# Stick-breaking attention: triangular matmuls against a backward VectorE scan

## The chip, the core and the metric

The kernel runs on one core of one Trainium2 chip. Five engines work from queues of their own and meet only through semaphores: TensorE (PE, with its weight loads shown as PEld), VectorE (DVE), ScalarE (ACT), GpSimd (POOL), and SyncE (SP), which here only starts transfers. The metric is the time of one execution on the device, in microseconds (us). Each engine runs its own instructions strictly in order, so an instruction that waits also holds back everything written behind it.

## What is computed

One transformer layer for 512 tokens of width 1024: RMSNorm, one projection, two kinds of attention (8 heads each, width 64), an output projection, a mixture of 32 experts with 4 chosen per token, and a last RMSNorm. The change touches only the stick-breaking heads:

```python
z = einsum('bhqd,bhkd->bhqk', q, k) * scale
strict = q_index > k_index
log_1mb = where(strict, log_sigmoid(-z), 0.0)
suffix = cumsum(log_1mb, axis=keys, reverse=True) - log_1mb
log_a = where(strict, log_sigmoid(z) + suffix, -inf)
out = einsum('bhqk,bhkd->bhqd', exp(log_a), v)
```

With sp = softplus(z) = -log_sigmoid(-z), log_a is z minus the sum of sp over this key and all later keys of the same query. A query tile of 128 sees only the keys up to its own end, so the four tiles of a head hold 128, 256, 384 and 512 keys.

## The kernel before, in words

Every fp32 operand of a matmul is split in two fp32r parts, high and low, and each product is three matmuls (high by high, high by low, low by high). ACT writes the high part, DVE subtracts it to get the low part.

The attention stage is one loop over steps `s` on every engine, 32 steps for 8 pairs of heads: steps 0 to 15 are stick-breaking (`STICK` is 16, four steps a pair), 16 to 31 are forgetting attention. I write i for `s % 4`. Between the attention instructions of a step stand the projection matmuls of later heads, cut in three parts of two or three units (a unit is three 512-column matmuls, L1618 to L1620); this is the fill. Functions `filled`, `finish`, `place` and `turn_part` fix before the run in which part each projection tile is worked on and where ACT and DVE empty it.

Before the change a stick-breaking step works with keys on the partitions:

- PE `z_scores(s)`: the mask matmul and three products a head (L1686, L1690) for two heads, into the PSUM pair `zpair[s % 2]`.
- ACT `softplus_tail(s)`: absolute value, exp, log (L832, L834, L836) of both heads at once into `lbuf`.
- DVE `softplus(s)`: adds max(z, 0) (L1205), copies to the fp32r `sp_hi` (L1210) and subtracts to `sp_lo` (L1211).
- PE `log_a(s-1)`: multiplies `sp_hi` and `sp_lo` of this and all later key tiles by a matrix of -1 (`neg_one`, or triangular `neg_tri`) and adds onto the scores (L1702).
- ACT `stick_exp(s-1)`: exp into `pbuf` (L844). DVE `stick_split(s-1)`: `av_hi`, `av_lo` (L1220, L1222).
- PE `pv_stick(s-2)`: six matmuls with v (L1717) into the PSUM pair `obank`.

After the fourth step of a pair ACT's `mix_evac(1, c)` (L878, L887) and DVE's `mix_lo_part(1, c)` (L1259, L1265) empty `obank`. The queues also hold, in every step but i=3, the split of a weight piece (L757 on ACT, L1127 on DVE) and the emptying of a projection tile (L804, L808, L817 on ACT; L1168, L1174 on DVE). The order on each engine is the order of the code.

Of the kernel before, what the change touches and what calls it, by code (L numbers as in the profile page):

```python
# [129 lines left out]
def build(nc, x, norm1_g, w_in, b_f, g_fox, g_sb, w_out, norm2_g, w_router, b_router, w1, b1, w2, b2,  # L130
# [6 lines left out]
    with ExitStack() as ctx:  # L137
# [27 lines left out]
        neg_tri = sb("neg_tri", [P, P], F32R)  # L165
        neg_one = sb("neg_one", [P, P], F32R)
# [43 lines left out]
        av_hi = in_slot("av_hi", [P, 2, 2, BANK], F32R, 4)  # L210
        av_lo = in_slot("av_lo", [P, 2, 2, BANK], F32R, 5)
# [20 lines left out]
        tri_raw = over("tri_raw", [P, P], F32, room_at)  # L232
        one_raw = over("one_raw", [P, P], F32, room_at + 512)
# [103 lines left out]
        absz, e_ready, ln_ready, sp_raw, sp_ready = (sem(n) for n in ("absz", "e_ready", "ln_ready", "sp_raw", "sp_ready"))  # L337
        loga_ready, a_ready, av_hi_r, av_lo_r, pvs_done = (sem(n) for n in ("loga_ready", "a_ready", "av_hi_ready", "av_lo_ready", "pvs_done"))
        mix_hi, mix_sq, mix_lo, sq_added = sem("mix_hi"), sem("mix_sq"), sem("mix_lo"), sem("sq_added")
        tri_ready = sem("tri_ready")  # L340
# [233 lines left out]
        def _(pool):  # L574
# [34 lines left out]
            constant(choose(maskS, [[1, P]], ALU.is_gt, MASKED, 0, -1))  # L609
# [140 lines left out]
        def _(act):  # L750
# [75 lines left out]
            def softplus_tail(s):  # L826

                n, l = (s % TT + 1) * P, lbuf[:, s % 2]
                act.wait_ge(scored, s + 1)
                if s >= 2:  # L830
                    act.wait_ge(sp_ready, s - 1)
                nc.scalar.activation(l[:, :, 0:n], zpair[s % 2][:, :, 0:n], ACT.Abs).then_inc(absz, 1)  # L832
                act.wait_ge(absz, s + 1)
                nc.scalar.activation(l[:, :, 0:n], l[:, :, 0:n], ACT.Exp, scale=-1.0).then_inc(e_ready, 1)  # L834
                act.wait_ge(e_ready, s + 1)
                nc.scalar.activation(l[:, :, 0:n], l[:, :, 0:n], ACT.Ln, bias=1.0).then_inc(ln_ready, 1)  # L836

            def stick_exp(s):
# [3 lines left out]
                if s >= 2:  # L842
                    act.wait_ge(av_lo_r, s - 1)
                nc.scalar.activation(pbuf[:, s % 2, :, 0:n], zpair[s % 2][:, :, 0:n], ACT.Exp).then_inc(a_ready, 1)  # L844

            def fox_exp(s):
# [4 lines left out]
                if u < 2:  # L851
                    act.wait_ge(av_lo_r, s - 1)
# [8 lines left out]
            def pt_evac(s):  # L861
# [3 lines left out]
                if u < TT:  # L865
                    act.wait_ge(loga_ready, STICK)
# [35 lines left out]
            act.wait_ge(consts, 22)  # L902
# [17 lines left out]
            for s in range(STEPS + 1):  # L920
                evacuate((s, True))
                if s > STICK and s % TT == 1 and s > STICK + TT:
                    mix_evac(0, (s - STICK - TT) // TT)
                if s < STICK:
# [10 lines left out]
                evacuate((s, False))  # L935
                if s == F_STEP + 1:
# [3 lines left out]
                if TT < s < STICK + TT and s % TT == 1:  # L940
                    mix_evac(1, s // TT - 1)
# [173 lines left out]
        def _(dve):  # L1115
# [80 lines left out]
            def sp_cols(i):  # L1196

                return slice(P * i * (i + 1) // 2, P * (i + 1) * (i + 2) // 2)

            def softplus(s):  # L1200

                i = s % TT
                n, l = (i + 1) * P, lbuf[:, s % 2]
                dve.wait_ge(ln_ready, s + 1)
                nc.vector.scalar_tensor_tensor(out=l[:, :, 0:n], in0=zpair[s % 2][:, :, 0:n], scalar=0.0,  # L1205
                                               in1=l[:, :, 0:n], op0=ALU.max, op1=ALU.add).then_inc(sp_raw, 1)
                dve.wait_ge(sp_raw, s + 1)
                if s >= TT:
                    dve.wait_ge(loga_ready, TT * (s // TT))
                chained(nc.vector.tensor_copy(sp_hi[:, :, sp_cols(i)], l[:, :, 0:n]))  # L1210
                nc.vector.tensor_tensor(sp_lo[:, :, sp_cols(i)], l[:, :, 0:n], sp_hi[:, :, sp_cols(i)].bitcast(F32),  # L1211
                                        ALU.subtract).then_inc(sp_ready, 1)

            def stick_split(s):

                n, b = (s % TT + 1) * P, s % 2
                dve.wait_ge(a_ready, s + 1)
                if s >= 2:
                    dve.wait_ge(pvs_done, s - 1)
                nc.vector.tensor_copy(av_hi[:, b, :, 0:n], pbuf[:, b, :, 0:n]).then_inc(av_hi_r, 1)  # L1220
                dve.wait_ge(av_hi_r, s + 1)
                nc.vector.tensor_tensor(av_lo[:, b, :, 0:n], pbuf[:, b, :, 0:n], av_hi[:, b, :, 0:n].bitcast(F32),  # L1222
                                        ALU.subtract).then_inc(av_lo_r, 1)
# [58 lines left out]
            for g in range(1, STAGES):  # L1282
                lo_early(g)
                if g == STAGES - 1:
                    dve.wait_ge(consts, 22)
                    chained(nc.vector.tensor_scalar(seltab[:, 0:E], iotas[:, 0:E], pmod, None, ALU.is_equal))
                    nc.vector.tensor_copy(neg_tri[:], tri_raw[:]).then_inc(tri_ready, 1)
                    nc.vector.tensor_copy(neg_one[:], one_raw[:]).then_inc(tri_ready, 1)
                    nc.vector.tensor_copy(sel8[:], sel_raw[:]).then_inc(tri_ready, 1)
# [27 lines left out]
            for s in range(STEPS + 1):  # L1317
                if s < STICK:
                    lower((s, True))
                    softplus(s)  # L1320
                elif s < STEPS:
                    fox_max(s)
                    lower((s, True))
                    fox_scale(s)
                else:
                    lower((s, True))
                if 1 <= s <= STICK:
                    stick_split(s - 1)
                elif s > STICK:
# [10 lines left out]
                if TT < s < STICK + TT and s % TT == 1:  # L1340
                    mix_lo_part(1, s // TT - 1)
# [273 lines left out]
        def _(pe):  # L1615
# [61 lines left out]
            def z_scores(s):  # L1677

                p, i = divmod(s, TT)
                j, n, zb, b = TT - 1 - i, (i + 1) * P, bank[2 * (s % 2):2 * (s % 2) + 2], p % 2  # L1680
                if s >= 2:
                    pe.wait_ge(a_ready, s - 1)
                if i == 0:
                    pe.wait_ge(proj_lo, 3 * p + 2)
                for m in range(2):
                    pe.matmul(zb[m][:, 0:P], identB[:], maskS, start=True, stop=False, skip_group_check=True)  # L1686
                for w, x in ((k_hi, q_hi), (k_hi, q_lo), (k_lo, q_hi)):
                    for m in range(2):
                        half = slice(64 * m, 64 * m + 64)
                        mm = pe.matmul(zb[m][:, 0:n], w[half, b, j * P:(j + 1) * P], x[half, b, j * P:S],  # L1690
                                       start=False, stop=w is k_lo, skip_group_check=True)
                mm.then_inc(scored, 1)

            def log_a(s):

                i, zb = s % TT, bank[2 * (s % 2):2 * (s % 2) + 2]
                pe.wait_ge(sp_ready, s + 1)
                for v in range(i + 1):
                    o, w = P * v * (v + 1) // 2, P * (v + 1)
                    for m in range(2):  # L1700
                        for part in (sp_hi, sp_lo):
                            mm = pe.matmul(zb[m][:, (i + 1) * P - w:(i + 1) * P], (neg_tri if v == i else neg_one)[:], part[:, m, o:o + w],  # L1702
                                           start=False, stop=v == i and part is sp_lo, skip_group_check=True)
                mm.then_inc(loga_ready, 1)

            def pv_stick(s):

                p, i = divmod(s, TT)
# [367 lines left out]
```

## Time and profile before

| quantity | value |
|---|---|
| median of 3 runs | 1536.88 us (1536.72 to 1537.83) |
| the profiled execution's own time | 1539.24 us |
| its span, first to last instruction | 1537.5 us |
| PE busy | 1482.2 us, 96% |
| DVE busy | 1335.3 us, 87% |
| ACT busy | 1108.4 us, 72% |
| stick-breaking scores begin / forgetting scores begin | 37.51 us / 166.34 us |

Busy shares are means over stages that differ. The attention stage lies between about 37 and 312 us, and from about 359 us on the expert weights stream through. A matmul in the timeline is shown with its whole pipeline (0.39 us for 512 columns), while the next one starts 0.23 us after it; what PE's queue pays for a matmul is the distance of starts, not its duration.

### The profile page before, as it was taken

To read this page: it belongs to the slowest core of one execution; us is meant where nothing else is said; L and a number is where in the kernel's file an instruction comes from. 1 tells how busy PE (TensorE), PEld (TensorE's weight loads), DVE (VectorE), ACT (ScalarE), POOL (GpSimd) and SP (SyncE) were. 2 spreads that over 40 slices of the span, in tenths; PEclk is the share of its full clock that TensorE was granted. 3 is DMA by queue.
4 is the path that set the end of the run, shared out by engine and by line. 5 is a ranking of instruction groups with operands and counts; after the bars stand their busy time and mean duration, and the time that the engine had idled before them with its cause. 6 is when DMAs were issued, how large, how long until landed. Compare 5 with 4: busy or idle time off the path is not lost.

```text
span 1537.5 us, 22435 instructions
## 1 busy us (share of the span) xinstructions
PE 1482.2 (96%) x7120; PEld 1196.7 (78%) x7120; DVE 1335.3 (87%) x1515; ACT 1108.4 (72%) x1314; POOL 257.0 (17%) x203
## 2 busy tenths in 40 slices
PE   6999998889899999999999999999999999999995
PEld 5788786777778788888888888778888888888874
DVE  5477655567999999999999999999999999999996
ACT  5466554254788888888888788888888888878875
POOL 5000000036011121111111211112221111111110
PEclk9999999999999999999999999999999999999998
DMA  8021121169999999999999999999999999999953
GB/s 249 13 82 44 40 82 56 32 231 368 344 368 372 361 363 373 378 351 368 366 377 366 366 366 367 366 359 376 357 376 358 364 374 363 370 372 360 358 200 120
DMA packets 100023, 451.82 MB, mean 294 GB/s; under 512 B 13394, under 2 KB 25682, under 8 KB 67216
## 3 DMA queue, kind: packets, MB, share of 16 engines
q1 hardware_dynamic: 90656, 434.68, 74.8%
q0 software_dynamic: 9328, 16.64, 4.5%
q8 instruction: 22, 0.36, 0.1%
q14 instruction: 17, 0.14, 0.0%
HBM read 445.18 MB, written 22.54 MB: 304 GB/s over the span
## 4 chain that ended last, share of the span: by engine, by line
PE 71%; DVE 17%; issue 7%; ACT 4%; POOL 1%; DVEq 0%; ACTq 0%; POOLq 0%
PE zpair L1979 43%; PE bank L1979 7%; DVE stage_lo L1127 7%; PE bank L1618 4%; PE bank L1619 3%; PE bank L1620 3%; ACT stage_hi L757 3%; DVE qk L1501 2%; DVE act_lo L1475 2%; DVE qk L1497 2%; PE bank L1949 2%; PE zpair L1702 1%; PE zpair L1958 1%; PE bank L1766 1%; PE bank L1717 1%
## 5 line engine op out<-in xcount | busy, mean ns | idle before, releaser
L1127 DVE TENSOR_TENSOR stage_lo<-ring,stage_hi 128x1024 fp32r<-128x1024 f32 x796 | 953.2, 1223 | 51.4 <-ACT stage_hi L757 12.2
L757 ACT CAST stage_hi<-ring 128x1024 fp32r<-128x1024 f32 x796 | 828.9, 1054 | 195.5 <-PE zpair L1979 149.4
L1979 PE MATMUL zpair<-stage_hi,act_hi 128*128 128x512 f32 x1024 | 323.5, 397 | 5.4 <-DVE stage_lo L1127 5.3
L1979 PE MATMUL zpair<-stage_lo,act_hi 128*128 128x512 f32 x1024 | 316.6, 390 | 0.0
L1979 PE MATMUL zpair<-stage_hi,act_lo 128*128 128x512 f32 x1024 | 316.4, 390 | 0.0
L1979 PEld LDWEIGHTS zpair<-stage_hi,act_hi 128*128 128x128 f32 x1024 | 187.4, 188 | 53.8 <-DVE stage_lo L1127 13.8
L1979 PEld LDWEIGHTS zpair<-stage_lo,act_hi 128*128 128x128 f32 x1024 | 192.8, 188 | 40.9
L1979 PEld LDWEIGHTS zpair<-stage_hi,act_lo 128*128 128x128 f32 x1024 | 192.7, 188 | 40.7
L1979 PE MATMUL bank<-stage_hi,act_hi 128*128 128x512 f32 x512 | 164.9, 403 | 7.0 <-DVE stage_lo L1127 4.5
L650 POOL COPY sidx<-gtab 128x1 int32 (+1 forms) x31 | 101.2, 3265 | 392.4 <-ACT qk L1030 392.4
L1979 PE MATMUL bank<-stage_lo,act_hi 128*128 128x512 f32 x512 | 159.2, 392 | 0.0
L1979 PE MATMUL bank<-stage_hi,act_lo 128*128 128x512 f32 x512 | 158.4, 391 | 0.0
L1979 PEld LDWEIGHTS bank<-stage_hi,act_hi 128*128 128x128 f32 x512 | 91.8, 189 | 36.0 <-DVE stage_lo L1127 16.5
L1979 PEld LDWEIGHTS bank<-stage_hi,act_lo 128*128 128x128 f32 x512 | 96.4, 188 | 21.3
L1979 PEld LDWEIGHTS bank<-stage_lo,act_hi 128*128 128x128 f32 x512 | 96.4, 188 | 20.9
L639 POOL COPY gidx<-gtab 128x1 int32 (+1 forms) x31 | 5.7, 185 | 487.4 <-PE bank L1943 487.4
L1475 DVE TENSOR_TENSOR act_lo<-bank,act_hi 128x512 fp32r<-128x512 f32 x128 | 81.9, 681 | 4.9 <-ACT act_hi L1016 3.3
L1618 PE MATMUL bank<-act_hi,stage_hi 128*128 128x512 f32 x192 | 80.2, 418 | 2.9 <-DVE v_lo L1168 2.7
L1619 PE MATMUL bank<-act_lo,stage_hi 128*128 128x512 f32 x192 | 75.8, 395 | 0.0
L1620 PE MATMUL bank<-act_hi,stage_lo 128*128 128x512 f32 x192 | 75.8, 395 | 0.0
L1022 ACT ACTIVATE qk<-qk 128x1024 f32<-128x1024 f32 x32 | 34.0, 1061 | 41.3 <-DVE qk L1497 41.3
L654 POOL DMA_INDIRECT x_scratch<-qk,sidx x31 | 58.3, 1880 | 25.0 <-POOL sidx L650 25.0
(310 smaller groups left out, 1483.7 us busy)
## 6 DMA issues: line engine op xcount, KB each, us to landing
ring<-in_w SPq DMA_DIRECT2D x384, 1024.0 KB, 7.5
ring<-in_w_in SPq DMA_DIRECT2D x12, 1024.0 KB, 5.4
ring<-in_w_out SPq DMA_DIRECT2D x4, 1024.0 KB, 4.8
xs_all<-in_x SPq DMA_DIRECT2D x4, 512.0 KB, 7.7
ring<-in_x SPq DMA_DIRECT2D x4, 512.0 KB, 3.8
tn_scratch<-qk SPq DMA_DIRECT2D x4, 512.0 KB, 2.9
x_scratch<-ring SPq DMA_DIRECT2D x4, 512.0 KB, 4.1
ring<-x_scratch SPq DMA_DIRECT2D x4, 512.0 KB, 5.6
```

Of the source, the lines that this page charges most:

```text
L650: nc.gpsimd.tensor_copy(sidx[:], gtab[:, i:i + 1] if isinstance(i, int) else gtab[:, bass.ds(i, 1)]).then_inc(sidx_copied, 1)
L654: nc.gpsimd.indirect_dma_start(out=x2_d[:, :], out_offset=bass.IndirectOffsetOnAxis(ap=sidx[:, 0:1], axis=0), in_=yout, in_offset=None, bo ...
L757: nc.scalar.copy(dst, src).then_inc(split_hi, 1)
L1022: nc.scalar.activation(sig, glu, ACT.Gelu_apprx_sigmoid).then_inc(sig_done, 1)
L1127: nc.vector.tensor_tensor(dst, src, hi_ap.bitcast(F32), ALU.subtract).then_inc(split_lo, 1)
L1475: nc.vector.tensor_tensor(dst_lo[:, 4 * h:4 * h + n, :], bank[6 + h][:, 0:n * P].rearrange("p (k t) -> p k t", k=n), dst_hi[:, 4 * h:4 * h ...
L1497: ins = nc.vector.tensor_scalar(glu[:, h * BANK:(h + 1) * BANK], bank[h][:], LIMIT, None, ALU.min)
L1501: ins = nc.vector.tensor_scalar(lin[:, h * BANK:(h + 1) * BANK], bank[2 + h][:], LIMIT, -LIMIT, ALU.min, ALU.max)
L1618: pe.matmul(dst, w_hi, m_hi, start=start, stop=False)
L1619: pe.matmul(dst, w_hi, m_lo, start=False, stop=False)
L1620: return pe.matmul(dst, w_lo, m_hi, start=False, stop=stop)
L1979: mm = pe.matmul(bank[b0 + h][:], w[:, k, :], m[:, j % STAGES, h * BANK:(h + 1) * BANK], start=start and w is T_hi and m is stage_hi, stop ...
```

## The change

Queries are put on the partitions and keys along the free dimension, as in the forgetting heads. `log_a` and its 160 matmuls go, with `sp_hi`, `sp_lo`, `av_hi`, `av_lo` and the two constant matrices. In their place:

- DVE `log_weights(s)`: adds max(z, 0) as before, then one `tensor_tensor_scan` a head that runs through the keys backward (step -1) and adds them up, then z minus the sum. It keeps fp32; no split.
- ACT `stick_exp(s)` now reads `lbuf` in SBUF.
- PE `turn_stick(s)`: two times i+1 transposes of `pbuf` into `obank`. It waits until DVE has emptied `obank` of the turned tile before (`st_lo_ready`), and for i=0 until the pair before has left it (`mix_lo`).
- ACT `stick_turned(s)` copies the turned tile to `pt_hi`, one instruction a head; DVE `stick_rest(s)` subtracts to `pt_lo`.
- PE `pv_stick(c)`: once a pair, 24 matmuls with v, with the same columns in all as the four calls before.
- `mix_evac` and `mix_lo_part` of a pair move from the end of the step with i=1 to the front of the step with i=2.

```diff
-            def log_a(s):
-                i, zb = s % TT, bank[2 * (s % 2):2 * (s % 2) + 2]
-                pe.wait_ge(sp_ready, s + 1)
-                for v in range(i + 1):
...
+            def turn_stick(s):
+                c, i = divmod(s, TT)
+                pe.wait_ge(a_ready, s + 1)
+                if i == 0:
+                    wait(pe, mix_lo, 2 * c)
+                else:
+                    pe.wait_ge(st_lo_r, s)
+                for m in range(2):
+                    for kb in range(i + 1):
+                        mm = pe.transpose(obank[m][:, kb * P:(kb + 1) * P], pbuf[:, s % 2, m, kb * P:(kb + 1) * P], identF[:])
+                mm.then_inc(st_turned, 1)
...
+            def pv_stick(c):
+                pe.wait_ge(st_lo_r, TT * (c + 1))
+                pe.wait_ge(proj_lo, 3 * c + 3)
+                weigh(c).then_inc(pvs_done, TT)
...
+            def log_weights(s):
+                n, l = (s % TT + 1) * P, lbuf[:, s % 2]
+                dve.wait_ge(ln_ready, s + 1)
+                chained(nc.vector.scalar_tensor_tensor(out=l[:, :, 0:n], in0=zpair[s % 2][:, :, 0:n], scalar=0.0,
+                                                       in1=l[:, :, 0:n], op0=ALU.max, op1=ALU.add))
+                for m in range(2):
+                    back = l[:, m, 0:n][:, ::-1]
+                    loose(nc.vector.tensor_tensor_scan(back, back, ones[:, 0:1].to_broadcast([P, n]), 0.0, ALU.add, ALU.mult))
+                dve.wait_ge(steps["dve"], count["dve"])
+                nc.vector.tensor_tensor(l[:, :, 0:n], zpair[s % 2][:, :, 0:n], l[:, :, 0:n], ALU.subtract).then_inc(loga_ready, 1)
...
+            def stick_rest(s):
                 i = s % TT
+                dve.wait_ge(st_hi_r, s + 1)
+                for m in range(2):
+                    ins = nc.vector.tensor_tensor(pt_lo[:, m, i:4 * i + 1:3, :], obank[m][:, 0:(i + 1) * P].rearrange("p (k q) -> p k q", q=P),
+                                                  pt_hi[:, m, i:4 * i + 1:3, :].bitcast(F32), ALU.subtract)
+                ins.then_inc(st_lo_r, 1)
...
             for s in range(STEPS + 1):
                 if s < STICK:
                     lower((s, True))
-                    softplus(s)
+                    if s % TT == 2 and s > TT:
+                        mix_lo_part(1, s // TT - 1)
+                    if s >= 2 and s % TT != 2:
+                        stick_rest(s - 2)
+                    log_weights(s)
...
                 if F_STEP <= s < F_STEP + 4 and s != F_STEP + 1:
                     forget_gate((0, None, 1, 2)[s - F_STEP])
-                if TT < s < STICK + TT and s % TT == 1:
-                    mix_lo_part(1, s // TT - 1)
+                if s % TT == 2 and s < STICK:
+                    stick_rest(s - 2)
...
                 for part in range(PARTS):
                     q = PARTS * s + part
-                    if part == 1 and 1 <= s <= STICK:
-                        log_a(s - 1)
+                    if s % TT == 1 and TT < s < STICK + TT and part == (1 if s > STICK else 2):
+                        pv_stick(s // TT - 1)
+                    if part == 2 and s % TT == 2 and s < STICK:
+                        turn_stick(s - 2)
...
+                if 1 <= s <= STICK and s % TT != 1:
+                    turn_stick(s - 1)
```

How the rows move is seen best in step 14, the third one with i=2 after a finished pair. On PE before, from the second part of the step on: the sums of `sp`, then fill, then the products with v of step 12 (after whose six rows come two units of fill and the scores of step 15).

```order
L1702 MATMUL zpair<-sp_hi,neg_one 128x128 [waits sp_ready]
L1702 MATMUL zpair<-sp_lo,neg_one 128x128
L1702 MATMUL zpair<-sp_hi,neg_one 128x128
L1702 MATMUL zpair<-sp_lo,neg_one 128x128
L1702 MATMUL zpair<-sp_hi,neg_tri 128x256
L1702 MATMUL zpair<-sp_lo,neg_tri 128x256
L1702 MATMUL zpair<-sp_hi,neg_tri 128x256
L1702 MATMUL zpair<-sp_lo,neg_tri 128x256
L1618 MATMUL bank<-act_hi,stage_hi 128x512 [waits proj_lo,split_lo]
```

On PE now, the last part of the same step and the start of step 15 (L1705 is `turn_stick`, L1687 the mask matmul of the next scores).

```order
L1705 MATMUL bank<-identF,pbuf 128x128 [waits mix_lo,a_ready]
L1705 MATMUL bank<-identF,pbuf 128x128
L1619 MATMUL bank<-act_hi,stage_hi 128x512
L1620 MATMUL bank<-act_lo,stage_hi 128x512
L1621 MATMUL bank<-act_hi,stage_lo 128x512
L1619 MATMUL bank<-act_hi,stage_hi 128x512
L1620 MATMUL bank<-act_lo,stage_hi 128x512
L1621 MATMUL bank<-act_hi,stage_lo 128x512
L1705 MATMUL bank<-identF,pbuf 128x128 [waits st_lo_ready,a_ready]
L1705 MATMUL bank<-identF,pbuf 128x128 x3
L1687 MATMUL zpair<-masks,identB 128x128 [waits loga_ready]
```

Two turned tiles stand in this one step with a single part of fill between them, and the second waits for DVE.

On DVE before, step 14 from the emptying of the pair (written at the end of step 13) on.

```order
L1259 SCALAR_TENSOR_TENSOR stick_lo<-bank,cols,stick_hi 64x512 [waits mix_sq] x2
L1265 TENSOR_TENSOR f_neg<-f_neg,f_max 128x512 [waits sq_added]
L1205 SCALAR_TENSOR_TENSOR lbuf<-zpair,lbuf 128x2x384 [waits ln_ready]
L1210 CAST sp_hi<-lbuf 128x2x384 [waits loga_ready,sp_raw]
L1211 TENSOR_TENSOR sp_lo<-lbuf,sp_hi 128x2x384 [waits dve_steps]
L1220 CAST av_hi<-pbuf 128x2x256 [waits pvs_done,a_ready]
L1222 TENSOR_TENSOR av_lo<-pbuf,av_hi 128x2x256 [waits av_hi_ready]
L1127 TENSOR_TENSOR stage_lo<-ring,stage_hi 128x1024 [waits split_hi]
L1174 SCALAR_TENSOR_TENSOR k_lo<-bank,k_hi 128x512 [waits scored,proj_hi]
```

On DVE now, the same stretch (L1209 is the scan, L1218 `stick_rest`).

```order
L1256 SCALAR_TENSOR_TENSOR stick_lo<-bank,cols,stick_hi 64x512 [waits mix_sq] x2
L1262 TENSOR_TENSOR f_neg<-f_neg,f_max 128x512 [waits sq_added]
L1205 SCALAR_TENSOR_TENSOR lbuf<-zpair,lbuf 128x2x384 [waits ln_ready]
L1209 SCALAR_TENSOR_TENSOR lbuf<-lbuf,ones 128x384 [waits dve_steps]
L1209 SCALAR_TENSOR_TENSOR lbuf<-lbuf,ones 128x384
L1211 TENSOR_TENSOR lbuf<-zpair,lbuf 128x2x384 [waits dve_steps]
L1132 TENSOR_TENSOR stage_lo<-ring,stage_hi 128x1024 [waits split_hi]
L1179 SCALAR_TENSOR_TENSOR k_lo<-bank,k_hi 128x512 [waits scored,proj_hi]
L1218 TENSOR_TENSOR pt_lo<-bank,pt_hi 128x128 [waits st_hi_ready]
L1218 TENSOR_TENSOR pt_lo<-bank,pt_hi 128x128
```

`stick_rest` of the tile with i=0, for which PE's second turn waits, stands last in DVE's step, behind `log_weights`, the weight piece and the projection tile. ACT's copy of that tile likewise stands last in ACT's step.

## Rows read from the trace of the kernel before

**Rows 1.** The page: span, busy time of each engine, the chain by engine.

```profile
span 1537.5 us, 22435 instructions
PE 1482.2 (96%) x7120; PEld 1196.7 (78%) x7120; DVE 1335.3 (87%) x1515; ACT 1108.4 (72%) x1314; POOL 257.0 (17%) x203
...
PE 71%; DVE 17%; issue 7%; ACT 4%; POOL 1%; DVEq 0%; ACTq 0%; POOLq 0%
```

**Rows 2.** Busy time by stretch: length, PE, PEld, DVE, ACT, POOL, clock, DMA share, GB/s.

```profile
119.65:150.69 31.04, 31.04 (x177) 25.33 (x176) 21.07 (x29) 18.99 (x28) 0.00 (x0) 1.00 0.12 35
37.51:63.75 26.24, 23.54 (x119) 18.60 (x119) 12.02 (x19) 11.62 (x18) 0.00 (x0) 0.93 0.09 32
63.75:95.45 31.70, 31.70 (x179) 26.05 (x179) 21.64 (x31) 19.80 (x29) 0.00 (x0) 1.00 0.22 67
...
157.50:181.73 24.23, 24.23 (x138) 19.97 (x137) 15.78 (x26) 11.89 (x21) 0.00 (x0) 1.00 0.13 44
```

**Rows 3.** The stretch of one pair, line L1702 (`log_a`) alone: length, PE, PEld.

```profile
119.65:150.69 31.04, 6.21 (x40) 5.60 (x40) 1.00 0.12 35
```

**Rows 4.** Timeline of PE, eight transposes of `turn_p` and the fill behind: start, us, what.

```profile
199.56 1.04 PE L1752 MATMUL zpair<-identF,pbuf 128*128 128x128 f32 x8
200.35 0.48 PE L1618 MATMUL bank<-act_hi,stage_hi 128*128 128x512 f32 x1
```

**Rows 5.** Timeline of PE, step 10: fill after `pv_stick`, scores, `log_a`; scores of step 11.

```profile
118.28 0.39 PE L1618 MATMUL bank<-act_hi,stage_hi 128*128 128x512 f32 x1
...
119.65 0.28 PE L1686 MATMUL zpair<-masks,identB 128*128 128x128 bf16 x2
...
122.09 0.22 PE L1702 MATMUL zpair<-sp_hi,neg_one 128*128 128x128 f32 x1
...
126.46 0.29 PE L1686 MATMUL zpair<-masks,identB 128*128 128x128 bf16 x2
```

**Rows 6.** Timeline of ACT, steps 10 and 11.

```profile
122.86 0.85 ACT L836 ACTIVATE lbuf<-lbuf 128x768 f32<-128x768 f32 x1
...
125.03 0.60 ACT L808 ACTIVATE k_hi<-bank 128x512 fp32r<-128x512 f32 x1
...
129.84 1.06 ACT L836 ACTIVATE lbuf<-lbuf 128x1024 f32<-128x1024 f32 x1
```

**Rows 7.** Timeline of DVE, step 10.

```profile
123.74 0.96 DVE L1205 SCALAR_TENSOR_TENSOR lbuf<-zpair,lbuf 128x768 f32<-128x768 f32 x1 [0.96 <-ACT lbuf L836]
...
127.27 1.22 DVE L1127 TENSOR_TENSOR stage_lo<-ring,stage_hi 128x1024 fp32r<-128x1024 f32 x1
128.40 0.68 DVE L1174 SCALAR_TENSOR_TENSOR k_lo<-bank,k_hi 128x512 fp32r<-128x512 f32 x1
```

**Rows 8.** Groups of DVE instructions by shape, 40 to 200 us: busy, mean ns.

```profile
L1211 DVE TENSOR_TENSOR sp_lo<-lbuf,sp_hi 128x768 fp32r<-128x768 f32 x4 | 3.8, 958 | 0.1
...
L1210 DVE CAST sp_hi<-lbuf 128x768 fp32r<-128x768 f32 x4 | 2.2, 560 | 0.1
...
L1187 DVE TENSOR_TENSOR_SCAN f_sum<-f_max,f_neg 128x512 f32<-128x512 f32 x1 | 1.2, 1217 | 0.0
...
L1248 DVE TENSOR_TENSOR pt_lo<-zpair,pt_hi 128x256 fp32r<-128x256 f32 x1 | 0.4, 415 | 0.0
```

**Rows 9.** Timeline of DVE, step 2: the first part of the forget gate.

```profile
64.12 0.75 DVE L1181 TENSOR_SCALAR f_sum<-bank,cols 128x512 f32<-128x512 f32 x1
...
65.51 0.42 DVE L1184 TENSOR_SCALAR f_max<-f_sum 128x512 f32<-128x512 f32 x1
```

**Rows 10.** Timeline of PE around its wait in step 0.

```profile
43.77 0.60 PE L1674 MATMUL bank<-identF,vT 128*128 128x128 f32 x4
47.07 0.76 PE L1618 MATMUL bank<-act_hi,stage_hi 128*128 128x512 f32 x1 [2.70 <-DVE v_lo L1168]
...
50.56 0.40 PE L1620 MATMUL bank<-act_hi,stage_lo 128*128 128x512 f32 x1
```

**Rows 11.** Busy time by stretch, as rows 2, behind that wait.

```profile
47.00:50.00 3.00, 2.93 (x7) 2.38 (x8) 0.52 (x1) 0.00 (x0) 0.00 (x0) 0.51 0.00 0
```

More of the change, by code:

```diff
@@ L842, in stick_exp, with stick_turned @@
                 if s >= 2:
-                    act.wait_ge(av_lo_r, s - 1)
-                nc.scalar.activation(pbuf[:, s % 2, :, 0:n], zpair[s % 2][:, :, 0:n], ACT.Exp).then_inc(a_ready, 1)
+                    act.wait_ge(st_turned, s - 1)
+                nc.scalar.activation(pbuf[:, s % 2, :, 0:n], lbuf[:, s % 2, :, 0:n], ACT.Exp).then_inc(a_ready, 1)
+            def stick_turned(s):
+                i = s % TT
+                act.wait_ge(st_turned, s + 1)
+                if s == 0:
+                    act.wait_ge(sel8_ready, 1)
+                if i == 0:
+                    wait(act, pvs_done, s)
+                for m in range(2):
+                    ins = nc.scalar.copy(pt_hi[:, m, i:4 * i + 1:3, :], obank[m][:, 0:(i + 1) * P].rearrange("p (k q) -> p k q", q=P))
+                ins.then_inc(st_hi_r, 1)
             def fox_exp(s):
@@ L923, in _ @@
                     mix_evac(0, (s - STICK - TT) // TT)
+                if s % TT == 2 and TT < s < STICK + TT:
+                    mix_evac(1, s // TT - 1)
+                if 2 <= s < STICK + 2 and (s - 2) % TT:
+                    stick_turned(s - 2)
                 if s < STICK:
@@ L1339, in _ @@
                     forget_gate((0, None, 1, 2)[s - F_STEP])
-                if TT < s < STICK + TT and s % TT == 1:
-                    mix_lo_part(1, s // TT - 1)
+                if s % TT == 2 and s < STICK:
+                    stick_rest(s - 2)
                 if s > STICK + TT and s % TT == 1:
@@ L1685, in z_scores @@
                 for m in range(2):
-                    pe.matmul(zb[m][:, 0:P], identB[:], maskS, start=True, stop=False, skip_group_check=True)
-                for w, x in ((k_hi, q_hi), (k_hi, q_lo), (k_lo, q_hi)):
+                    pe.matmul(zb[m][:, i * P:(i + 1) * P], identB[:], maskS, start=True, stop=False, skip_group_check=True)
+                for w, x in ((q_hi, k_hi), (q_hi, k_lo), (q_lo, k_hi)):
                     for m in range(2):
                         half = slice(64 * m, 64 * m + 64)
-                        mm = pe.matmul(zb[m][:, 0:n], w[half, b, j * P:(j + 1) * P], x[half, b, j * P:S],
-                                       start=False, stop=w is k_lo, skip_group_check=True)
+                        mm = pe.matmul(zb[m][:, 0:n], w[half, b, i * P:(i + 1) * P], x[half, b, 0:n],
+                                       start=False, stop=w is q_lo, skip_group_check=True)
@@ new lines, in weigh @@
+            def weigh(ph):
+                for kb in range(TT):
+                    for m in range(2):
+                        for w, x in ((v_hi, pt_hi), (v_hi, pt_lo), (v_lo, pt_hi)):
+                            mm = pe.matmul(obank[m][:, kb * P:S], w[:, ph % 2, kb, :],
+                                           x[:, m, 4 * kb:3 * kb + TT, :].rearrange("p i q -> p (i q)"),
+                                           start=kb == 0 and w is v_hi and x is pt_hi, stop=kb == TT - 1 and w is v_lo, skip_group_check=True)
+                return mm
@@ L1762, in pv_fox @@
                     pe.wait_ge(ms_read, 1)
-                for kb in range(TT):
-                    for m in range(2):
-                        for w, x in ((v_hi, pt_hi), (v_hi, pt_lo), (v_lo, pt_hi)):
-                            mm = pe.matmul(obank[m][:, kb * P:S], w[:, ph % 2, kb, :],
-                                           x[:, m, 4 * kb:3 * kb + TT, :].rearrange("p i q -> p (i q)"),
-                                           start=kb == 0 and w is v_hi and x is pt_hi, stop=kb == TT - 1 and w is v_lo, skip_group_check=True)
-                mm.then_inc(pvf_done, 1)
+                weigh(ph).then_inc(pvf_done, 1)
             def sums(kind):
```

98 lines of the change are left out of this document (23 added, 75 removed).

## The prediction, made before the changed kernel ran

> **What bounds the kernel now.** I read the page first: PE is busy 96% of the span and carries 71% of the chain that ended last [rows 1]. A mean over stages says little about one stage, so next came the busy time by stretch. One pair of stick-breaking heads takes 31.04 us, from the scores of step 10 to those of step 14; PE is busy all of it, DVE 21.07 and ACT 18.99 [rows 2]. So each microsecond of PE's queue counts there, and DVE and ACT have 10 and 12 us to spare, as long as PE never waits for them. Then I read the three queues side by side over one step, since the change trades PE work for a longer way through ACT and DVE. A late attention stage is not caught up later: nearly everything behind it hangs on PE too, so I pass the difference on in full.
>
> **What PE gains.** `log_a` goes. Its 40 matmuls a pair are 6.21 us of busy time [rows 3]. They stand in four runs, and each run's last matmul shows 0.39 us where the next starts 0.23 us later (six starts in 1.37 us [rows 5]), so the queue pays 6.21 - 4 x 0.17 = 5.5 us. Twenty transposes a pair come: eight take 0.79 us of the queue [rows 4], so twenty take 2.0. `pv_stick` keeps 24 matmuls a pair and their columns, the scores theirs; I cost both at nothing, being moved on the same engine. If PE never waited, a pair would take 31.04 - 5.5 + 2.0 = 27.5 us, 3.5 less.
>
> **What DVE and ACT get.** Eight subtractions (958 ns at 768 columns [rows 8], 0.83 at the mean width of 640) and eight casts (560 ns at 768, about 0.49) go: 10.5 us a pair. Eight scans come. One forward scan of 512 columns took 1217 ns [rows 8]; at the mean of 320 columns that is 0.82, so 6.5 us. Four subtractions come, 3.3, and eight from PSUM for `pt_lo` (415 ns at 256 columns [rows 8], so about 0.48), 3.9. DVE goes from 21.1 to 24.3 us a pair; ACT gets eight copies, about 3.4 us, and goes to 22.4. Both still fit under 27.5: it is not their work but its place that matters.
>
> No row shows a backward scan or one with a broadcast second operand. Below I bound it by the subtraction of as many columns, 0.69 us at 512; above by twice the forward scan, 2.43. I take the forward scan's 1.22, the nearest row, the same instruction on fp32 in SBUF.
>
> **The wait that comes.** In a step with i=2, PE turns the tile i=0 ahead of its last part of fill, and the tile i=1 right behind that part. `turn_stick` for i=1 waits until DVE has emptied `obank` of the first tile. I follow both sides from the end of `pv_stick`, at 118.28 in step 10 [rows 5].
>
> - ACT empties the pair and then makes abs, exp and log of the new scores: the log ends at 122.86 + 0.85 = 123.71, 5.4 us after the start [rows 6]. DVE now works through max 0.96, two scans of 384 columns 0.95 each, subtraction 0.96 and two handovers 0.1: 3.9. Behind it stand the weight piece (128.40 - 127.27 = 1.1) and the projection tile, 0.65 [rows 7], then the two `pt_lo` subtractions of 128 columns, about 0.28 each. Together 5.4 + 3.9 + 1.1 + 0.7 + 0.6 = 11.7 us. ACT's copy of that tile is ready before this: `k_hi` ends at 125.63 [rows 6], 7.4, and half a microsecond more.
> - PE has fill, scores and a part of fill, 122.09 - 118.28 = 3.8 [rows 5], a second part 1.4, the first turn 0.2, the third part 1.4: 6.8 us.
>
> PE waits 11.7 - 6.8 = 4.9 us. Behind the waiting transpose are queued the scores of the next step, hence ACT's whole next step, so nothing overtakes. The pair takes 27.5 + 4.9 = 32.4 us, 1.4 more than now. The other new waits fall short: from the scores of i=3 the log is done after 129.84 + 1.06 - 126.46 = 4.4 us [rows 5, 6], the log weights after 9.5, the exp after 10.6, and PE comes to that turn after 11.3; the pair's last `pt_lo` is done after 15.3, and PE comes to `pv_stick` after 16.4. This bites three times, in steps 6, 10 and 14: 4.2 us.
>
> **The two ends.** In step 2 no pair has to be emptied, but the first part of the forget gate stands between `log_weights` and `stick_rest`. It begins at 64.12 before [rows 9]; PE's queue loses 0.4 us of `log_a` ahead, and DVE's 3.6 us of softplus and split become 3.9, so it begins at about 64.0, lasts 65.51 + 0.42 - 64.12 = 1.8 us [rows 9], then 0.6 for `pt_lo`, 0.4 for the turn. Step 3 starts at 66.8 instead of 63.75 [rows 2]: 3.1 us later. In step 5 the forget gate's last part delays the squares of the first pair, 0.5 more. From step 15 to 18, PE loses two `log_a` runs (4.2 us) and three `pv_stick` calls (3.1), gains one of 3.75 and 14 transposes, 1.5, and meets waits of 0.9 for the copy of v and 1.7, since the last stick-breaking exp now stands behind the first forgetting exp and DVE's longer log weights: -4.2 - 3.1 + 3.75 + 1.5 + 2.6 is 0.6 on the 24.23 [rows 2]. I give 0.5 of this back in the first forgetting steps, where other waits stand: 0.1.
>
> **The clock.** After a wait of 2.70 us in step 0 the granted clock was 0.51 for 3 us, the 1.2 GHz level [rows 10, 11]. Eight starts took 50.56 - 47.07 = 3.5 us where eight take 1.8 at full clock: 1.6 lost. The new waits are longer, so I add 1.6 four times, 6.4 us; PE stands on the way to every next wait, so the loss isn't hidden.
>
> The Trainium skill (TensorE: Matmul & The Clock Gate, "What's actually happening") advises against such a term: "For modeling, the ramp penalty is <1% of a typical kernel span". By it the sum below would be 7.9 and the time 1544.8. The trace agrees on the size, for 6.4 of 1537.5 us is 0.4%, but against a change of 8 us that is no small term, and I keep it.
>
> **Sum.** 3.1 + 4.2 + 0.5 + 0.1 + 6.4 = 14.3 us. The profiled execution took 1539.24 us, 2.4 more than the median of the runs, so it becomes 1553.5; for the median, 1536.88 + 14.3 = 1551.2. I predict 1551.
>
> **Rivals.**
>
> - PE stays full (the side of faster). Mechanism: `stick_rest` of i=0 is done before PE has finished the third part of fill. It decides at 6.8 us after `pv_stick`, where I find 11.7. Then PE's gain stands: four pairs at 3.5, 14 us, 1523. For it speaks that DVE and ACT have room in every pair; against it that the log alone ends after 5.4 us and DVE's four instructions after another 3.9, both in front of it. Even free scans leave 9.8. Chance 0.08.
> - The wait comes, the clock does not fall, for instance because the PE queue's short work around it is enough. 14.3 - 6.4 = 7.9: 1545. Against it: after 2.70 us it fell. Chance 0.17.
> - Scans at the upper bound. `log_weights` at i=2 grows by 1.6 us, and at i=3 by 2.4, which passes the 0.7 us of room before that turn and adds 1.7: 3.3 a pair, 13 us more: 1564. Chance 0.09. At the lower bound, scans of 384 columns cost 0.55 and each wait shrinks by 0.8: 1548, inside the forecast's own spread.
> - The delay is absorbed, since a later wait (a transfer, a POOL step before the experts) ends at the same time as before: 1537. Against it: in the expert stage PE carries most of the chain. Chance 0.04.
>
> **Numbers.** The forecast has 0.60, and its own spread is 1546 to 1556: scans at the lower bound and waits 0.5 us off at four places. The 0.02 left is for what I don't see. For 8 in 10, the range takes in the case without the clock (1545, less 2) and stops short of the dear scans: 1543 to 1558. About 0.2% is what a measurement of this kernel tells from no change, 3 us. Faster by more: the first rival, 0.09 with a little of the unseen. Within: 0.05. Slower: 0.86.
>
> **What the new profile would show.** PE idle four times, in steps 2, 6, 10 and 14, each time before a transpose into `obank` and released by DVE's `pt_lo` subtraction, 4 to 5.5 us; a granted clock near 0.5 behind each; pairs 34 us apart. The scans at 0.95 us for 384 columns. DVE at 24 us a pair. PE without these waits in steps 3 to 5. I am wrong if PE is full from 60 to 180 us (then the first rival), if the idle time before these transposes is under 3 us, or if scans take over 2 us.

## The result, and the profile after

The changed kernel takes 1552.06 us (median of 4 runs, 1551.10 to 1554.38); the kernel before took 1536.8 us beside it (4 runs, 1535.03 to 1537.83). The ratio is 1.010, with a 95% interval of 1.0085 to 1.0115: slower by 15.3 us, where 14.3 were predicted.

The page of the changed kernel, against [rows 1]: span, busy times, and further down the chain by engine.

```profile
span 1549.2 us, 22311 instructions
...
PE 1476.2 (95%) x7040; PEld 1190.0 (77%) x7040; DVE 1345.4 (87%) x1529; ACT 1118.9 (72%) x1346; POOL 265.0 (17%) x200
...
PE 68%; DVE 19%; issue 7%; ACT 5%; POOL 0%; DMA 0%; DVEq 0%; ACTq 0%; POOLq 0%
```

PE is busy 6 us less and the span is 11.7 us longer: about 18 us more in which PE does nothing. The waits of PE in the attention stage say where (engine, tile and line <- releaser: us in total, times, longest).

```profile
PE bank L1705 <- DVE pt_lo L1218: 17.5, 4, 4.5
PE bank L1619 <- DVE ring L1275: 4.5, 2, 4.2
PE bank L1619 <- DVE v_lo L1173: 3.1, 2, 2.7
PE zpair L1737 <- DVE pt_lo L1245: 2.5, 2, 2.1
PE bank L1619 <- DVE stage_lo L1132: 2.4, 1, 2.4
```

The first row is new, and it is the whole surplus. The others have their like in the kernel before. Four times, in steps 2, 6, 10 and 14, the transposes of the tile i=1 (L1705) wait for the subtraction `pt_lo` (L1218) of the tile i=0, for 4.27, 4.20, 4.52 and 4.51 us.

Step 10 on three engines, in the order PE, DVE, ACT. These answer [rows 5], [rows 7] and [rows 6]; each is a timeline (start, us, what, and in brackets the idle time before and its releaser).

```profile
129.25 0.38 PE L1705 MATMUL bank<-identF,pbuf 128*128 128x128 f32 x2
...
130.63 0.40 PE L1621 MATMUL bank<-act_hi,stage_lo 128*128 128x512 f32 x1
135.54 1.09 PE L1705 MATMUL bank<-identF,pbuf 128*128 128x128 f32 x4 [4.52 <-DVE pt_lo L1218]
136.42 0.42 PE L1687 MATMUL zpair<-masks,identB 128*128 128x128 bf16 x2
```

```profile
129.48 0.96 DVE L1205 SCALAR_TENSOR_TENSOR lbuf<-zpair,lbuf 128x768 f32<-128x768 f32 x1 [0.96 <-ACT lbuf L825]
130.47 1.81 DVE L1209 TENSOR_TENSOR_SCAN lbuf<-lbuf,ones 128x384 f32<-128x384 f32 x2
132.31 0.96 DVE L1211 TENSOR_TENSOR lbuf<-zpair,lbuf 128x768 f32<-128x768 f32 x1
133.18 1.22 DVE L1132 TENSOR_TENSOR stage_lo<-ring,stage_hi 128x1024 fp32r<-128x1024 f32 x1
134.32 0.68 DVE L1179 SCALAR_TENSOR_TENSOR k_lo<-bank,k_hi 128x512 fp32r<-128x512 f32 x1
134.92 0.48 DVE L1218 TENSOR_TENSOR pt_lo<-bank,pt_hi 128x128 fp32r<-128x128 f32 x2
```

```profile
128.60 0.85 ACT L825 ACTIVATE lbuf<-lbuf 128x768 f32<-128x768 f32 x1
...
131.30 0.42 ACT L844 CAST pt_hi<-bank 128x128 fp32r<-128x128 f32 x2
136.67 0.65 ACT L844 CAST pt_hi<-bank 128x256 fp32r<-128x256 f32 x2 [4.95 <-PE bank L1705]
```

PE turned the first tile at 129.25 and was through its fill at 131.0. ACT's copy of that tile started at 131.30. From then on the tile only waited for its place in DVE's queue: `log_weights`, the weight piece and the projection tile ran first, without a gap, and the subtraction that PE needed began at 134.92.

The busy time by stretch (length, PE, PEld, DVE, ACT, POOL, clock, DMA share, GB/s), against [rows 2] and [rows 11]: the pair from step 10 to 14, and 3 us behind the wait.

```profile
125.44:159.71 34.27, 29.75 (x156) 23.69 (x155) 23.52 (x33) 21.60 (x36) 0.00 (x0) 0.90 0.12 34
...
136.00:139.00 3.00, 3.00 (x13) 1.90 (x13) 0.76 (x2) 1.18 (x3) 0.00 (x0) 0.50 0.00 0
```

A pair takes 34.27 us instead of 31.04 (from step 3 to 7 it is 34.24, from 7 to 11 it is 34.16). PE is busy 29.75 us of it although it got less to do, because part of it runs at the 1.2 GHz level: the granted clock was 0.50 behind the waits in steps 2, 10 and 14, and 0.57 in the 3 us behind that in step 6.

The scans and the subtractions from PSUM, by shape (busy, mean ns), against [rows 8].

```profile
L1209 DVE TENSOR_TENSOR_SCAN lbuf<-lbuf,ones 128x512 f32<-128x512 f32 x8 | 9.4, 1211 | 0.1
L1209 DVE TENSOR_TENSOR_SCAN lbuf<-lbuf,ones 128x384 f32<-128x384 f32 x8 | 7.2, 945 | 0.1
...
L1218 DVE TENSOR_TENSOR pt_lo<-bank,pt_hi 128x256 fp32r<-128x256 f32 x8 | 3.0, 420 | 7.3 <-ACT pt_hi L844 7.3
```

A backward scan with a broadcast operand costs what the forward scan did: 1211 against 1217 ns at 512 columns.

### The profile page after: what moved, and what is told of

Its sections match the earlier page's. It is cut to its first block, busy times and chain, and to the rows that moved or that the text cites. A ratio compares the mean times of both kernels' runs of the same rounds, so it can differ in the third digit from the quotient of the medians.

```text
span 1549.2 us, 22311 instructions
## 1 busy us (share of the span) xinstructions
PE 1476.2 (95%) x7040; PEld 1190.0 (77%) x7040; DVE 1345.4 (87%) x1529; ACT 1118.9 (72%) x1346; POOL 265.0 (17%) x200
## 4 chain that ended last, share of the span: by engine, by line
PE 68%; DVE 19%; issue 7%; ACT 5%; POOL 0%; DMA 0%; DVEq 0%; ACTq 0%; POOLq 0%
PE zpair L1978 43%; DVE stage_lo L1132 7%; PE bank L1978 7%; PE bank L1619 3%; ACT stage_hi L746 3%; PE bank L1620 2%; PE bank L1621 2%; DVE qk L1502 2%; DVE act_lo L1476 2%; DVE qk L1498 2%; PE bank L1948 2%; PE bank L1713 2%; PE zpair L1957 1%; DVE lbuf L1209 1%; PE zpair L1691 1%
## 5 line engine op out<-in xcount | busy, mean ns | idle before, releaser
L639 POOL COPY sidx<-gtab 128x1 int32 (+1 forms) x31 | 109.3, 3527 | 392.1 <-ACT qk L1035 392.1
```

What stands on the lines that cost most here:

```text
L639: nc.gpsimd.tensor_copy(sidx[:], gtab[:, i:i + 1] if isinstance(i, int) else gtab[:, bass.ds(i, 1)]).then_inc(sidx_copied, 1)
```

## The experiments

Two theories stood against each other on the cause. *Place*: the wait comes from where DVE's subtraction stands in its queue, and the lower clock behind it is a cost of its own. *Work*: DVE (or ACT) simply has too much to do in this version. And one question on the gain: does PE's queue bound the stage at all?

### The subtraction and the copy moved up

On ACT the copy of the tile i=0 goes from the end of the step to right behind the log; on DVE its subtraction goes from the end of the step to ahead of `log_weights`.

```diff
                     softplus_tail(s)
                 elif s < STEPS:
                     fox_exp(s)
+                if s % TT == 2 and s < STICK:
+                    stick_turned(s - 2)
...
-                if s % TT == 2 and s < STICK:
-                    stick_turned(s - 2)
...
-                    if s >= 2 and s % TT != 2:
+                    if s >= 2:
                         stick_rest(s - 2)
                     log_weights(s)
...
-                if s % TT == 2 and s < STICK:
-                    stick_rest(s - 2)
```

> The changed kernel with stick_turned of the tile i=0 on ACT right behind softplus_tail, and stick_rest of it on DVE ahead of log_weights. My theory (place, not work): the low part of that tile is ready about 6.5 us after pv_stick instead of 11.3, PE comes to its turn after 6.7, so the four waits of 4.2 to 4.5 us nearly go (under 0.5 us each), the clock stays up, a pair takes 27.6 us instead of 34.2, and the whole 1552 - 17.5 - 6.4 = 1528 us, or up to 1531 if the clock falls at later waits instead. Rival (DVE and ACT are too full for a pair of 27.6 us): the wait moves to the turns of i=2 and i=3 or to pv_stick, a pair takes 30 to 32 us, the whole 1540 to 1548.

Measured: 1530.63 us (5 runs, 1529.46 to 1531.53), ratio to the kernel before 0.9951 (0.9938 to 0.9965). The first view is the waits of PE from 60 to 155 us, the second the busy time of two pairs.

```profile
PE bank L1673 <- ACT vT L793: 1.1, 1, 1.1
PE bank L1617 <- DVE k_lo L1179: 0.7, 1, 0.7
PE bank L1617 <- DVE v_lo L1173: 0.5, 1, 0.5
```

```profile
84.57:113.09 28.52, 28.43 (x159) 22.93 (x159) 23.01 (x33) 21.42 (x36) 0.00 (x0) 1.00 0.22 72
113.09:141.50 28.41, 27.87 (x156) 22.36 (x155) 23.14 (x33) 21.30 (x36) 0.00 (x0) 1.00 0.16 45
```

All four waits are gone, DVE does the same 23 us a pair, and the clock stays full. This is a *place* result: no work was removed, and 21 us came back. From step 0 to step 20 the two profiles differ by 23.2 us (148.74 against 171.92); 1.5 of these are not the move's but come in steps 0 and 1, where the clock behind a wait that both have happened to stay full in one and not in the other (last section). The pairs are 0.8 to 0.9 us longer than the 27.6 expected: three short waits are left, 2.3 us together, and the first of the two pairs has more fill. The version is faster than both kernels, by 0.5% against the one before. DVE's timeline in step 10 of this version:

```profile
117.79 0.49 DVE L1218 TENSOR_TENSOR pt_lo<-bank,pt_hi 128x128 fp32r<-128x128 f32 x2 [1.62 <-ACT pt_hi L844]
118.19 0.95 DVE L1205 SCALAR_TENSOR_TENSOR lbuf<-zpair,lbuf 128x768 f32<-128x768 f32 x1
119.17 1.81 DVE L1209 TENSOR_TENSOR_SCAN lbuf<-lbuf,ones 128x384 f32<-128x384 f32 x2
```

DVE is now the one that waits, 1.62 us for ACT's copy, and has that time to spare. Both instructions were moved here; the subtraction alone was not tried. In the changed kernel the copy was done at 131.72, 0.7 us after PE had come to its turn, so with the copy left late some wait would have stayed.

### Half the way, and the copy alone

Here both pieces stand only ahead of the weight piece and the projection tile, behind `log_weights` (the copy behind `stick_exp`):

```diff
                 if s > STICK:
                     pt_lo_part(s - 1)
+                if s % TT == 2 and s < STICK:
+                    stick_rest(s - 2)
                 for g in range(6, TILES + 4):
```

> The changed kernel with the copy and the low part of the tile i=0 moved only ahead of the weight piece and the projection tile, still behind log_weights. Place theory: the chain behind pv_stick is shorter by the 1.15 + 0.65 us of those two (in step 2 by the 1.8 us of the forget gate), so each of four waits is 2.6 us instead of 4.4, 7 us in all: 1545. If the clock no longer falls after a wait of 2.6 us, up to 6 more: 1539. Rival (something else ends the wait): 1552.

Measured: 1541.14 us (10 runs, 1538.69 to 1545.18), ratio 1.0023 (1.0013 to 1.0032). PE's waits from 60 to 165 us:

```profile
PE bank L1705 <- DVE pt_lo L1218: 10.5, 4, 2.8
```

2.6 us each, as expected: the two DVE instructions taken out of the way (in step 2 the forget gate's part) were worth 1.7 to 1.9 us of every wait. The total lies between the two figures expected, 1545 with the low clock and 1539 without, and so does the clock: over the 3 us behind the four waits it read 0.69, 0.50, 0.53 and 1.00. The next kernel moves ACT's copy alone to its early place and leaves DVE as it was; its edit is the part on `stick_turned` of the first experiment:

> The changed kernel with ACT's copy of the turned tile i=0 moved up, right behind the log, and DVE's subtraction left where it is. Theory (the subtraction is late because of what DVE does ahead of it, the copy was ready long before): four waits of 4.2 to 4.5 us as in the changed kernel, 1552 us. Rival (ACT's place makes the wait): the waits shrink to under 2 us, 1543 us or less.

Measured: 1554.16 us (4 runs, 1549.58 to 1555.22), ratio 1.0115 (1.0098 to 1.0132). PE's waits from 35 to 330 us:

```profile
PE bank L1705 <- DVE pt_lo L1218: 17.5, 4, 4.5
```

The same 17.5 us as in the changed kernel, and a median 2.1 us above it. ACT's late place costs nothing as long as DVE's is later: it is DVE's that makes the wait.

### PE kept busy during the wait

```diff
+                if s % TT == 2 and s < STICK:
+                    pe.wait_ge(loga_ready, s)
+                    keep_busy(2 * ((s + 1) % 2), 34)
                 if 1 <= s <= STICK and s % TT != 1:
                     turn_stick(s - 1)
```

> The changed kernel with 34 small matmuls (3.7 us of PE's queue) into an unused PSUM bank in each of the four waits. Theory (the clock is a term of its own): the granted clock stays at 1.00 behind the waits, and 1.6 us each come back, 1545.5. Rival (the clock costs nothing since DVE's chain hides it): 1552.

Measured: 1543.82 us (5 runs, 1542.16 to 1544.98), ratio 1.0038 (1.0024 to 1.0051). Busy time by stretch, the pairs from step 7 to 11 and from 11 to 15:

```profile
100.44:132.69 32.25, 31.46 (x192) 25.57 (x190) 23.42 (x33) 21.49 (x35) 0.00 (x0) 1.00 0.10 32
132.69:164.97 32.28, 31.50 (x191) 25.60 (x189) 23.42 (x33) 21.49 (x35) 0.00 (x0) 1.00 0.24 68
```

`keep_busy` issues matmuls of 256 columns. The transposes still start when `pt_lo` lets them (in step 10, 10.10 us after the scores in both kernels), and of the waits 0.5 to 0.8 us are left. PE's waits from 60 to 165 us:

```profile
PE bank L1705 <- DVE pt_lo L1218: 2.6, 4, 0.8
```

The clock now reads 1.00, and the same stretches take 32.25 and 32.28 us instead of 34.16 and 34.27. Each of these stretches, though, also ends with the slow transposes of the next wait, 0.4 us. What the clock costs behind one wait is seen from the waiting transpose to the scores of the next step with i=2 (for the last, to those of step 18):

| wait in step | changed kernel | PE kept busy | difference |
|---|---|---|---|
| 2 | 67.14 to 91.33: 24.19 us | 66.99 to 89.48: 22.49 us | 1.70 |
| 6 | 101.79 to 125.44: 23.65 us | 99.98 to 122.12: 22.14 us | 1.51 |
| 10 | 135.54 to 159.71: 24.17 us | 132.22 to 154.42: 22.20 us | 1.97 |
| 14 | 169.81 to 195.74: 25.93 us | 164.51 to 189.22: 24.71 us | 1.22 |

Together 6.4 us, as much as predicted; where it is less than 2, part of it went into short waits that showed up once PE was faster (0.5 us for the copy of v behind the last), or the clock was low for less long (step 6). From step 0 to step 20 the version is 6.3 us shorter (165.61 against 171.92), its span 6.0. The medians differ by 8.2; the other 2 us lie in how the profiled executions stand to their medians, 1.2 above and 1.0 below.

### DVE's work, less and more

The scans left out (the suffix sums are missing, so the router picks other experts, further expert passes run, and the total of 2128.46 us can't be compared; the attention stage can):

```diff
-                for m in range(2):
-                    back = l[:, m, 0:n][:, ::-1]
-                    loose(nc.vector.tensor_tensor_scan(back, back, ones[:, 0:1].to_broadcast([P, n]), 0.0, ALU.add, ALU.mult))
```

> The changed kernel without the scans (the sum over later keys is left out). This takes 6.5 us of DVE's work from each pair. Place theory: only the two scans in step i=2 stand in the chain, 1.8 us, so waits are 2.6 us and the whole 1552 - 7 = 1545 (1539 if the clock no longer falls). Rival (DVE's work is the bound): up to 26 us, 1526.

Measured, first PE's waits from 60 to 165 us, then the busy time from step 7 to 11:

```profile
PE bank L1702 <- DVE pt_lo L1215: 10.1, 4, 2.7
```

```profile
96.97:127.88 30.91, 28.17 (x157) 22.70 (x155) 17.54 (x25) 21.38 (x35) 0.00 (x0) 0.98 0.10 32
```

DVE did 5.9 us less in this pair (17.54 against 23.42), and the waits (2.52, 2.07, 2.74, 2.74) each lost only about the 1.8 us of the two scans that stand ahead of them, 2.1 in step 6. PE still waits with a DVE that is idle for 13 us of a pair. The work theory would have had the waits go.

The other way round, each scan run once more, into a spare buffer:

```diff
                     back = l[:, m, 0:n][:, ::-1]
+                    chained(nc.vector.tensor_tensor_scan(spare[:, 0:n][:, ::-1], back, ones[:, 0:1].to_broadcast([P, n]), 0.0, ALU.add, ALU.mult))
```

> The changed kernel with each backward scan run once more into a spare buffer ahead of the real one. Theory: what DVE does ahead of the subtraction lengthens PE's wait one for one. In the steps with i=2 two scans of 384 columns come, 1.9 us, so the four waits go from 4.4 to 6.3 us; in the steps with i=3 two of 512, 2.4 us, of which 0.7 has room, so 1.7 more: 3.6 us a pair, 14 us, 1566 us. Rival (the scans lie beside other work): waits as before, 1552 us.

Measured: 1572.5 us (4 runs, 1571.43 to 1578.14), ratio 1.0242 (1.0218 to 1.0265). PE's waits from 35 to 330 us:

```profile
PE bank L1707 <- DVE pt_lo L1220: 27.1, 4, 7.8
PE bank L1621 <- DVE v_lo L1174: 7.8, 4, 2.7
```

Three of the four waits are 6.28, 6.52 and 6.49 us, the 4.4 of before plus the two extra scans. The fourth, in step 6, is 7.77: there the forget gate's last part, behind the longer scans of step 5, also held up ACT, which waited 2.07 us for it while it emptied the first pair, and so came to the log later. But I had expected 3.6 us a pair and got 6.1 and 6.3 (40.25 and 40.52 us for the pairs from step 6 and 10, against 34.11 and 34.27). The place I named for the rest, the turn of i=3, shows no wait at all. Instead PE waited for `v_lo`, 2.19 us in step 13: DVE's delay came out at a tile of the projections, which I had not followed. Waits explain 4.2 of the 6.3 us. The other 2.1 are PE's own time, 31.81 us busy instead of 29.75 for the same 156 matmuls: the mean clock of the stretch was 0.87 instead of 0.90, and it was also low behind the wait for `v_lo` (0.54 over 3 us). In the pair before it is 4.4 and 1.8. So the total is 1572, not 1566.

### What PE's queue is worth

In the kernel before, the products with `sp_lo` left out, 20 of the 40 sum matmuls of a pair (the sums lose their low part):

```diff
-                        for part in (sp_hi, sp_lo):
+                        for part in (sp_hi,):
```

> The kernel before with 20 of its 40 sum matmuls a pair left out (the products with the low part of softplus; the sums lose their low part). Theory that PE's queue bounds the stick-breaking stage of the kernel before: each pair loses 5.5 / 2 = 2.75 us, pairs of 28.3 us instead of 31.04, four pairs 11 us, 1526 us. Rival, that DVE or ACT bounds it as much: pairs stay at 31, PE shows new waits, 1537 us.

Measured: 1527.31 us (4 runs, 1525.45 to 1528.11), ratio 0.9935 (0.9918 to 0.9951). The pair from step 10 to 14:

```profile
113.90:142.19 28.29, 28.29 (x157) 22.66 (x156) 20.99 (x29) 18.76 (x28) 0.00 (x0) 1.00 0.12 38
```

28.29 us, 2.75 less than 31.04, to the hundredth what half of 5.5 is. The total fell by 9.8 us, where 11 were expected. PE is still never idle in this pair. The conversion of busy time into queue time, 6.21 to 5.5, holds.

And in the version with copy and subtraction moved up, every transpose issued twice:

```diff
-                for m in range(2):
+                for m in (0, 1, 0, 1):
                     for kb in range(i + 1):
```

> The kernel with copy and subtraction of tile i=0 moved up (1530.6 us), every transpose of the turned tiles issued twice. Theory that PE's queue bounds the stage again once the wait is gone: 20 more transposes a pair at 0.1 us, 2.0 us a pair, pairs of 30 us, 8 us in all, 1538.5 us. Rival (DVE and ACT set the pace there by now): under 0.5 us a pair, 1531 to 1533 us.

Measured: 1532.51 us (6 runs, 1531.59 to 1534.42), ratio 0.9973 (0.9960 to 0.9985).

```profile
86.38:116.82 30.44, 30.44 (x179) 25.17 (x179) 23.09 (x33) 21.51 (x36) 0.00 (x0) 1.00 0.21 66
116.82:146.62 29.80, 29.80 (x177) 24.63 (x176) 23.23 (x33) 21.51 (x36) 0.00 (x0) 1.00 0.14 39
```

PE's busy time in these two pairs grew from 56.30 to 60.24 us, 1.97 a pair: twenty transposes cost the predicted 2.0. The pairs grew by 1.9 and 1.4, the rest filled small waits. From the first scores to step 20 this version is 7.0 us later than the one with single transposes (155.77 against 148.74); 1.6 of these come before the first turned tile, from the clock in steps 0 and 1, so the transposes cost 5.5 us where 8 were expected. PE's queue bounds the stage, but not all of it.

The total is only 1.9 us more, which by itself would have spoken for the rival. Most of the missing part lies at the very end: behind the last start of an expert matmul into `zpair` (L1976) the span goes on for 52.9 us with single transposes, and for 49.9 with double ones. There the granted clock differs. Busy time by stretch of the last 48 expert matmuls, first with single transposes, then with double ones:

```profile
1494.29:1508.28 13.99, 13.99 (x48) 10.97 (x48) 9.51 (x9) 6.58 (x7) 0.10 (x1) 0.78 0.53 171
```

```profile
1499.30:1511.94 12.64, 12.63 (x48) 9.98 (x48) 9.50 (x9) 6.59 (x7) 0.10 (x1) 0.88 0.58 189
```

Both follow a wait of 3.74 us, and the same matmuls take 1.35 us longer at the lower clock. Behind them the mean clock is 0.72 and 0.78, and 1.7 us more are lost. So the profiles tie these 3 us to the clock, the first part of them outright; why it stayed low longer in one of them is open, and no run tested it.

## Why the prediction was right

It named the mechanism, the four places and the size of each wait. That the total came within 1 us is in part luck: in the profiles the attention stage grew by 12.2 us instead of 14.3, and about 3 us of the medians' difference come from elsewhere. By its own steps:

- **PE's queue, 27.5 us a pair without waits.** 27.87 us busy at full clock in the version without the four waits. Right within 0.4; its two parts were confirmed by themselves (2.75 and 1.97 us).
- **The wait, 4.9 us.** Measured 4.20 to 4.52. From the end of `pv_stick` (124.02) the log ended after 5.4 us, as predicted, `log_weights` took 3.8 for 3.9, and the last `pt_lo` was done after 11.4 for 11.7. PE came after 7.0 for 6.8. The 0.4 us is in these two small differences. The size of the wait is a difference of two long ways, so this is as near as it gets.
- **The first pair's end, 3.1 us.** Steps 0 to 3 took 29.62 us instead of 26.24 [rows 2], 3.4 more; 0.4 of it is the four transposes behind the wait at the low clock, which the prediction counted under the clock.
- **The clock, 1.6 us four times.** Measured 1.70, 1.51, 1.97 and 1.22, together 6.4 as predicted. The cost of one wait is up to 2.0: in step 10, PE was busy 29.75 us in a pair instead of the 27.87 of the version without waits. The term was read from fill alone at half speed, while here the transposes and scores of the next step run slow too; that some of it is absorbed by later waits brings the sum back to 6.4, which I had not foreseen ("PE stands on the way to every next wait, so the loss isn't hidden"). The rival without the term, 1545, is 7 us off. The Trainium skill (TensorE: Matmul & The Clock Gate, "What's actually happening") has the penalty under 1% of a span, and so it is: 6.3 of 1549.2 us are 0.4%. They are also half of the 12.2 us that the stage grew.
- **A pair, 34.0 us** (27.5 + 4.9 + 1.6). Measured 34.24, 34.16, 34.27, from step 3, 7 and 11 on. The first of them is 2.5 us more than before, not 3.5: the 0.5 for the forget gate in step 5 didn't show, and that pair had been 31.70 us long [rows 2], not 31.04.
- **The last end, 0.1 us.** Step 15 to 18 took 25.05 us for 24.23 [rows 2], +0.8; the next two steps gave 1.0 back. The 0.6 and the -0.5 were right in sign, but this stretch also holds the clock's cost behind the fourth wait, 1.2 us, so without that it was better than I said by 1.5 us. This and the clock's smaller cost there are the largest part of the 2.1 us between 14.3 and 12.2.

From step 0 to step 20 the changed kernel is 12.2 us longer in its profiled execution. The step 0 itself began 0.9 us later, which isn't the change: the same start shows up at 37.5 or at 38.2 to 38.4 us in kernels that are alike up to there. Step 28 gave 2.6 back: the profiled execution of the kernel before ran part of it slow and that of the changed kernel didn't. Busy time by stretch, first the kernel before, then the changed one, the same step:

```profile
259.92:273.41 13.49, 13.23 (x65) 10.97 (x64) 5.39 (x9) 3.72 (x7) 0.00 (x0) 0.79 0.16 47
```

```profile
273.55:284.49 10.94, 10.66 (x64) 8.95 (x63) 5.39 (x9) 3.72 (x7) 0.00 (x0) 1.00 0.22 71
```

The same matmuls, 13.49 us at a mean clock of 0.79 and 10.94 at 1.00. The profiled execution of the kernel before was 2.4 us over its median, that of the changed kernel 1.0 under its own, which is nearly all of why the spans differ by 11.7 us and the medians by 15.3. The prediction added its terms to the median; against the two spans alone the 14.3 is 2.6 us too high, against the medians 1.0 too low.

**The rivals.** PE full: the point it named, `stick_rest` done before 6.8 us, was missed by 4.6. Its gain exists, though, and the moved copy and subtraction collect part of it: 11.0 us from step 0 to step 20 (148.74 against 159.76), of which some 1.5 are the clock in steps 0 and 1, and 6.9 in the total. Dear scans: 945 ns at 384 columns rules them out; run twice, they cost 20 us, where the rival had 13. Absorbed: the first expert matmul starts 10.8 us later (369.6 against 358.8), and nothing behind it makes up for that.

## What to carry to other kernels

When work leaves the engine that bounds a stage, look first at where the new, longer path stands in the queues of the others, not at their busy shares: here DVE had 10 us to spare in every 34 and still made PE wait 4.5, and moving two subtractions ahead of six other instructions (and ACT's copy with them) turned 1% slower into 0.5% faster. (A second pair of PSUM banks for the turned tiles would lift the same wait; it was not tried.) Find the wait by timing both sides from one common event up to the instruction that meets, and price the clock behind it apart. Work that fills the wait is no gain in itself, but with a clock that falls it was worth 6 us in the profiles and 8 in the medians.

## What the runs showed of the hardware

- Whether the clock falls behind a wait of 2 to 3 us differs between executions. In step 0, the same wait of 2.70 us for `v_lo` was followed, over the next 3 us, by a clock of 0.50 in the kernel before and in the changed one, of 0.53 to 0.74 in six others, and of 1.00 in two: copy and subtraction moved up, and the copy alone. The version with double transposes has both moved up too and read 0.72, so it isn't the move. First the changed kernel, then the version with copy and subtraction moved up, 3 us from the end of that wait:

```profile
47.90:50.90 3.00, 2.95 (x7) 2.40 (x8) 0.50 (x1) 0.00 (x0) 0.00 (x0) 0.50 0.00 0
```

```profile
47.80:50.80 3.00, 2.92 (x14) 2.25 (x14) 0.53 (x1) 0.00 (x0) 0.00 (x0) 1.00 0.00 0
```

  Seven matmuls in one, fourteen in the other. Behind the half-way version's waits of 2.42, 2.52, 2.78 and 2.79 us it was 0.69, 0.50, 0.53 and 1.00; behind those of 2.52, 2.07, 2.74 and 2.74 us without the scans it was 0.57, 1.00, 0.50 and 0.54. Behind the four waits of 4.2 to 4.5 us of the changed kernel it fell each time (0.50, 0.60, 0.50, 0.50). One profile is no safe ground for a clock term of a short wait, nor for a difference of 1.5 us between two kernels.
- A scan of 512 columns costs the same backwards and with a broadcast second operand (1211 ns) as forwards on two full operands (1217 ns, the only width at hand). The backward one took 945 ns at 384 columns, 678 at 256 and 412 at 128.
- Kernels that differ only in the attention stage ended 49.9 to 52.9 us after the start of their last expert matmul into `zpair`, at a mean clock of 0.88 and 0.82 in the two extremes, so a microsecond or two of a total can come from there.
